# A hybrid attention and expert layer on one core: modulation rows, earlier head turns, products with diagonals, and one gather per tile

## The chip, the cores and the metric

The kernel runs on one core of a Trainium2 chip. The metric is device time in microseconds of one execution, the median of several. A profiled execution has a time of its own, which is given beside its span. The engines are TensorE (PE, and PEld for its weight loads), VectorE (DVE), ScalarE (ACT), GpSimd (POOL) and the DMA queues, which SyncE (SP), ScalarE and GpSimd issue.

## What is computed

One layer on 512 tokens of width 1024, in float32. `rms_norm(x)` is scaled and shifted by rows of `ada = c @ w_ada + b_ada`, projected by `w_in`, and goes through two attentions: a windowed one with 8 query heads and 2 key heads of 64 (chunks of 64, a window of two chunks, a bias by distance, a sink), and a latent one with 8 heads of 96 over all earlier chunks. Both are softmax attentions. Then comes a product-key expert network over 16384 experts.

```python
ada = c @ w_ada + b_ada
shift1, scale1, gate1, shift2, scale2, gate2 = [t[:, None, :] for t in jnp.split(ada, 6, axis=-1)]
h = rms_norm(x, norm1_g) * (1.0 + scale1) + shift1
z = h @ w_in
...
p = jnp.exp(scores - m)
denom = jnp.sum(p, axis=-1, keepdims=True) + jnp.exp(sink - m)
o = jnp.einsum('bckgqs,bcskd->bcqkgd', p / denom, vb)        # windowed
...
p = jax.nn.softmax(s, axis=-1)                               # latent, v alike
...
mix = jnp.concatenate([out_a, out_b], axis=-1).astype(x.dtype) @ w_out
x = x + gate1 * mix
h2 = rms_norm(x, norm2_g) * (1.0 + scale2) + shift2
x = x + gate2 * peer_ffn(h2, peer_w_query, peer_sub_keys, peer_u, peer_v)
```

`peer_ffn` scores 8 heads of keys, takes the 16 best of 128 twice and the 16 best pairs, and sums `gelu(u_e . x) * v_e` over them with softmax weights.

## The kernel before

It is one hand-written program per engine. Each engine has its list of instructions, and semaphores join them (`wait_ge`, `then_inc`); the order within an engine is the order in which the code is written. An engine that waits holds back all that stands behind it.

**Start.** SP loads c, x and then the weights in chunks of 512 columns (2 MB): first the modulation chunks 2, 3, 0 and 1 (`ada_order`), then the chunks of `w_in`. Chunks 2, 0 and 1 are `prepared`: DVE multiplies them by c and sums over the rows of 128 (`modulate`, L1243 and L1245), and PE sums over partitions (`modulation`, L874). Chunk 3 is `direct`: PE multiplies its columns with c, 32 matmuls of one moving column (L885). GpSimd adds the squares of x (L523), PE sums them over partitions (L897), ACT takes the root (L598), DVE the reciprocal (L1232). DVE scales (L1266), ACT shifts (L601), and `z_tile` (L915) is the projection by `w_in`.

**Heads.** Per token tile tt of 128: `project` makes the latent queries and keys, ACT copies them, DVE rotates and norms them (`rope`, `sum_heads`, `norm_heads`, which ends with the gain multiply L1364), and `turn_heads` transposes them on PE, 4 heads to a bank of PSUM, two banks in turn, each copied by ACT (`copy_heads`, L661). `turn_queries` does the same for the windowed queries (L942, `copy_queries`).

**Attention** is a pipeline of 48 units: 16 windowed ones (one token tile, two heads, at most 256 keys) and then 32 latent ones (one token tile, one head, 128 to 512 keys). In pass u PE does `scores(u + 2)` (L1002 windowed, over 64 rows; L1005 latent, over 96), `transposes(u)` (L1015, one 128x128 tile per 128 keys and head: 2 or 4 in a windowed unit, 1 to 4 in a latent one, 56 and 80 in all) and `values(u - 1)` (L1032). DVE does `bias_and_max`, divides the exponentials by their sum in place (`scale_probs`, L1417 reciprocal and L1420 multiply) and copies the result out. ACT does the exponentials (L716) and copies the transposed tiles to SBUF (L726). GpSimd has nothing to do here.

**Keys and experts.** Key scores of four token tiles go to SBUF by ACT (L790); three of them (p = 1 to 3) go out to HBM through two buffers, so that the copy of p = 3 waits until that of p = 1 has left. Then come 128 tiles of the table u and 128 of v. ACT rounds each (`high`), GpSimd makes the rest for u (`low_u`, L539), and PE makes 24 matmuls of 352 columns (`dot`, L1145 to L1147). Meanwhile DVE searches the keys of p = 0, then of p = 1 to 3 (`search`), and between the steps of a search it makes dot products with 128 gathered rows (`row_dot`, L1516) for the last token tile. GpSimd issues these gathers (L552) between its `low_u`; seven row buffers are there, and a gather waits until DVE has used the row seven before it (`row_used`). At u tile 28 PE turns the result of the search of p = 1 (`turn_slots`, L1163, which waits for DVE) and then builds gates (L1156) for 16 tiles. The rule for gathers is:

```python
while g < 2 * SU and (row_step[g - NROWS] <= m - 2 if g >= NROWS else m >= S0 + 3 + g):
    gather(g)
```

Of the kernel before, what the change touches and what calls it, by code (L numbers as in the profile page):

```python
# [59 lines left out]
def build(nc, xT, c, positions, position_cols, w_ada, b_ada, norm1_g, norm2_g, w_in, swa_q_norm, swa_k_norm,  # L60
          swa_sinks, mla_q_a_norm, mla_kv_a_norm, mla_w_uq, mla_w_ukv, mla_q_norm, mla_k_norm,
          w_out, peer_w_query, sub_keys, u_tiles, u_rows, v_tiles, outT):
    ctx = ExitStack()
    with ctx:
# [7 lines left out]
        def region(start, entries):  # L72
# [12 lines left out]
        (res, ident, ones, iota, cT, b_cols, ada, g1, g2, gs, eps), at0 = region(BASE, [  # L85
# [3 lines left out]
            ("g1", [P, KD], F32), ("g2", [P, KD], F32), ("gs", [P, KD], F32), ("eps", [P, 1], F32)])  # L89
# [16 lines left out]
            ("g_mla", [P, 2, QK], F32), ("trig", [P, TT, 2, ROPE // 2], F32), ("posq", [P, TT], I32),  # L106
# [11 lines left out]
        accs = m2[:].rearrange("p a h d -> p (a h d)")[:, 1024:2048].rearrange("p (a c) -> p a c", a=2)  # L118
        zsq_k = qkT[:].rearrange("p a t -> p (a t)")[:, 0:TT * P].rearrange("p (t c) -> p t c", t=TT)
# [25 lines left out]
        sout = (sout0, sout1)  # L145
# [55 lines left out]
        ms1 = sem("ms1")  # L201
        sd1 = sem("sd1")
        ada_done = sem("ada_done")
        ada_read = sem("ada_read")
        h_scaled = sem("h_scaled")
# [29 lines left out]
        p_ready = sem("p_ready")  # L235
        pt_ps = sem("pt_ps")
# [83 lines left out]
        direct = [ada_order[1]]  # L320
# [5 lines left out]

        def chunk(n):
            at = slot[n][0]
            return ring[at][:] if at < 3 else spare[at - 3]

        NSMALL = 12
# [83 lines left out]
        def _(sp):  # L415
# [38 lines left out]
            for p in range(1, TT):  # L454
                sp.wait_ge(s_copied, p + 1)
                sp.dma_start(keys[p], sout[p % 2][:].rearrange("p a n -> p (a n)")).then_inc(s_out[p % 2], 16)
# [51 lines left out]
        def _(pool):  # L508
            nc.gpsimd.memset(eps[:], EPS)
# [24 lines left out]

            sum_squares(rstd2[:], h2T, sq2, sq2_sum, KD - 1)
# [31 lines left out]
        def _(act):  # L567
# [20 lines left out]
            act.dma_start(g_mla[:, 0, :], mla_q_norm.partition_broadcast(P)).then_inc(small_in, 16)  # L588
            act.dma_start(g_mla[:, 1, :], mla_k_norm.partition_broadcast(P)).then_inc(small_in, 16)
# [8 lines left out]
            nc.scalar.activation(rstd1, ps[:, 6, :], ACT.Sqrt, bias=eps[:], scale=1.0 / D).then_inc(sd1, 1)  # L598
            for k in range(KD):
# [1132 lines left out]
```

## Time and profile before

| what | value |
|---|---|
| median of 3 runs | 1495.8 us (1495.46 to 1496.79) |
| profiled execution, its own time | 1498.02 us |
| its span | 1496.2 us |
| PE busy, share of the span | 1416.0 us, 95% |
| DVE, ACT, POOL busy | 1223.2, 707.6, 740.8 us |
| mean granted TensorE clock | 0.968 |

The span runs from the first to the last instruction. PEclk is the TensorE clock that was granted, as a share of 2.4 GHz; 0.50 is 1.2 GHz. Ends of matmuls are modelled, so that pieces of PE overlap in the rows; starts are what to go by.

### The profile page before, as it was taken

The page shows a single profiled execution, that of the slowest core. Times are in us where ns is not written, and L with a number is a line of the kernel's source. Part 1 is how long each engine was busy: PE and PEld are TensorE (multiplying, and loading weights), DVE is VectorE, ACT ScalarE, POOL GpSimd, SP SyncE. Part 2 cuts the span into 40 slices and gives each one's busy share as a digit, 9 for nine tenths or more (in the row PEclk, how much of TensorE's full clock was granted, in tenths as well). Part 3 has the DMA queues.
Part 4 walks back from the last instruction along what each step waited for, and adds up shares of the span by engine and source line. Part 5 has one row for each costly group of instructions (what it writes and reads, how often), then busy time and mean ns, then how long its engine had stood idle before and what let it go on. Part 6 is the DMA issues. An engine that isn't in the chain of part 4 may idle for free.

```text
span 1496.2 us, 23503 instructions
## 1 busy us (share of the span) xinstructions
PE 1416.0 (95%) x8439; PEld 1309.5 (88%) x8439; DVE 1223.2 (82%) x2649; ACT 707.6 (47%) x1311; POOL 740.8 (50%) x472
## 2 busy tenths in 40 slices
PE   3899899989897999989999999899999999999999
PEld 2564566768897999989999998899999999999998
DVE  3867667865779988958898886569999999999997
ACT  2234546332542688448853883343344334443342
POOL 2001000020467878768777776855555555565540
PEclk9999559999998999999999999999999999999999
DMA  8740100263569999999999999989999999999996
GB/s 319 278 147 1 57 1 1 80 234 137 189 224 333 319 330 334 358 380 321 325 345 402 329 332 351 412 288 372 391 396 386 395 392 391 389 393 392 391 390 228
DMA packets 158259, 438.88 MB, mean 293 GB/s; under 512 B 16768, under 2 KB 50880, under 8 KB 156992
## 3 DMA queue, kind: packets, MB, share of 16 engines
q1 hardware_dynamic: 91488, 244.55, 45.4%
q0 software_dynamic: 46080, 167.79, 29.4%
q10 hardware_dynamic: 20576, 25.05, 4.7%
q8 instruction: 67, 1.10, 0.3%
q14 instruction: 48, 0.39, 0.1%
HBM read 390.11 MB, written 47.22 MB: 292 GB/s over the span
## 4 chain that ended last, share of the span: by engine, by line
PE 75%; DVE 11%; DMA 5%; POOL 5%; ACT 2%; issue 2%; ACTq 0%; SPq 0%; DVEq 0%; POOLq 0%
PE ps L1196 11%; PE ps L1197 11%; PE ps L1198 11%; PE ps L1145 6%; PE ps L1146 6%; PE ps L1147 6%; PE ps L1156 5%; PE ps L915 4%; POOL lo L539 3%; PE ps L1032 2%; DMA raw<-in_u_tiles 2%; PE ps L1002 2%; PE ps L1015 2%; PE ps L1005 1%; POOL row_res L552 1%
## 5 line engine op out<-in xcount | busy, mean ns | idle before, releaser
L779 ACT ACTIVATE hi<-raw 128x1024 fp32r<-128x1024 f32 x256 | 271.2, 1060 | 312.0 <-PE ps L1198 221.7
L539 POOL TENSOR_TENSOR lo<-raw,hi 128x1024 fp32r<-128x1024 f32 x122 | 294.3, 2418 | 146.7 <-ACT hi L779 139.8
L1145 PE MATMUL ps<-h2hi,hi 128*128 128x352 f32 x1024 | 340.2, 332 | 26.2 <-POOL lo L539 17.2
L1146 PE MATMUL ps<-h2lo,hi 128*128 128x352 f32 x1024 | 334.8, 327 | 0.0
L1147 PE MATMUL ps<-h2hi,lo 128*128 128x352 f32 x1024 | 334.3, 327 | 0.0
L1197 PE MATMUL ps<-clo,hi 128*128 128x352 f32 x1008 | 324.1, 322 | 0.0
L1196 PE MATMUL ps<-chi,hi 128*128 128x352 f32 x1008 | 324.1, 322 | 0.0
L1198 PE MATMUL ps<-chi,lo 128*128 128x352 f32 x1008 | 324.1, 322 | 0.0
L1145 PEld LDWEIGHTS ps<-h2hi,hi 128*128 128x128 f32 x1024 | 196.4, 192 | 30.0 <-POOL lo L539 19.2
L552 POOL DMA_INDIRECT row_res<-in_v_tiles,E x91 | 149.9, 1647 | 137.3 <-DVE y_tok L1651 105.8
L1147 PEld LDWEIGHTS ps<-h2hi,lo 128*128 128x128 f32 x1024 | 196.2, 192 | 0.0
L1146 PEld LDWEIGHTS ps<-h2lo,hi 128*128 128x128 f32 x1024 | 196.1, 192 | 0.0
L1196 PEld LDWEIGHTS ps<-chi,hi 128*128 128x128 f32 x1008 | 189.3, 188 | 0.0
L1198 PEld LDWEIGHTS ps<-chi,lo 128*128 128x128 f32 x1008 | 189.3, 188 | 0.0
L1197 PEld LDWEIGHTS ps<-clo,hi 128*128 128x128 f32 x1008 | 189.3, 188 | 0.0
L1638 DVE TENSOR_TENSOR lo<-raw,hi 128x1024 fp32r<-128x1024 f32 x128 | 156.4, 1222 | 20.4 <-issue 10.0
L552 POOL DMA_INDIRECT rows<-in_v_tiles,E x69 | 111.6, 1617 | 84.1 <-DVE y_tok L1651 68.3
L803 ACT ACTIVATE act_out<-ps 128x352 f32<-128x352 f32 x128 | 59.2, 463 | 148.9 <-PE ps L1147 113.2
L1516 DVE SCALAR_TENSOR_TENSOR row_res<-row_res,ps 128x1024 f32<-128x1024 f32 x91 | 108.7, 1215 | 11.0 <-DMA row_res<-in_u_rows,E 5.8
L552 POOL DMA_INDIRECT row_res<-in_u_rows,E x91 | 90.5, 995 | 38.8 <-DVE row_res L1516 18.5
L814 ACT ACTIVATE ohW<-eqI,wS 128x128 f32<-128x128 f32 x352 | 107.4, 391 | 0.0
L1651 DVE SCALAR_TENSOR_TENSOR y_tok<-row_res,cc,y_tok 128x1024 f32<-128x1024 f32 x72 | 92.2, 1280 | 1.9
(286 smaller groups left out, 2216.2 us busy)
## 6 DMA issues: line engine op xcount, KB each, us to landing
raw<-in_u_tiles SPq DMA_DIRECT2D x128, 512.0 KB
raw<-in_v_tiles SPq DMA_DIRECT2D x128, 512.0 KB
gelus<-act_out ACTq DMA_DIRECT2D x128, 176.0 KB
act_in<-gelus SPq DMA_DIRECT2D x128, 176.0 KB
gates<-stage SPq DMA_DIRECT2D x32, 512.0 KB
gate<-gates SPq DMA_DIRECT2D x32, 512.0 KB
late<-in_w_ada SPq DMA_DIRECT2D x4, 2048.0 KB, 8.5
qkT<-in_w_ada SPq DMA_DIRECT2D x3, 2048.0 KB, 14.3
```

Of the source, the lines that this page charges most:

```text
L539: nc.gpsimd.tensor_tensor(lo[m % 3][:], raw[m % 3][:], hi[m % 3][:].bitcast(F32), ALU.subtract).then_inc(u_lo, 1)
L552: nc.gpsimd.indirect_dma_start(rows[g % NROWS], None, table, bass.IndirectOffsetOnAxis(ap=at, axis=0)).then_inc(row_in[g % NROWS], 16)
L779: nc.scalar.activation(hi[m % 3][:], raw[m % 3][:], ACT.Copy).then_inc(t_hi, 1)
L814: last = nc.scalar.activation(ohW[half][:, t, :], eqI[:, half, t, :], ACT.Copy, scale=wS[:, col:col + 1])
L1145: nc.tensor.matmul(out, hi[n % 3][:, cols], dense(h2hi, k), start=(k == 0), stop=False)
L1146: nc.tensor.matmul(out, hi[n % 3][:, cols], dense(h2lo, k), start=False, stop=False)
L1147: last = nc.tensor.matmul(out, lo[n % 3][:, cols], dense(h2hi, k), start=False, stop=(k == KD - 1))
L1196: nc.tensor.matmul(out, hi[m % 3][:, cols], chi[n % 4][:], start=(n == 0), stop=False)
L1197: nc.tensor.matmul(out, hi[m % 3][:, cols], clo[n % 4][:], start=False, stop=False)
L1198: last = nc.tensor.matmul(out, lo[m % 3][:, cols], chi[n % 4][:], start=False, stop=False)
L1516: nc.vector.scalar_tensor_tensor(out=row, in0=row, scalar=1.0, in1=x_tok, op0=ALU.mult, op1=ALU.mult, accum_out=aa[:, g:g + 1]).then_inc(r ...
L1638: tt_(lo[m % 3][:], raw[m % 3][:], hi[m % 3][:].bitcast(F32), ALU.subtract).then_inc(v_lo, 1)
```

## The change

There are seven edits.

1. **Modulation rows.** Chunks 3 and 1 (`direct`) are now multiplied by PE as rows: c is the stationary operand (one column), and 512 columns of the chunk move, 8 matmuls for a chunk. ACT copies the row to SBUF, and four matmuls of one row and one column turn it into columns. DVE prepares chunks 2 and 0 alone. The sum of squares comes first on PE. DVE computes the scale as soon as chunks 2 and 3 are there, and scales six of eight parts before it waits for the shift.
2. **Tables.** ACT loads the tables for Sqrt and Gelu with a one-element activation ahead of their use.
3. **Heads turned sooner.** `turn_heads(1)` stands ahead of `z_tile(0, 3)`, and the scores of units 0 and 1 ahead of the last turns. The gain of the latent heads is multiplied in ACT's copy of the turned queries, not by DVE.
4. **Products with diagonals.** DVE inverts the sums only. GpSimd writes `ident * (1 / sum)`, one 128x128 tile per head, and PE multiplies the exponentials with it by ordinary matmuls where it transposed.
5. **Key copies.** p = 1, 2 and 3 have a buffer each, so ACT's copies wait for no transfer.
6. **Gathers.** At most one per u tile until tile 28, at most three from there.
7. The modulation of `gate1` and `scale2` on DVE is moved behind the attention, and the Gelu of the gathered sums on ACT (L855) one tile later.

```diff
-        direct = [ada_order[1]]
+        direct = [ada_order[1], ada_order[3]]
...
+            def diagonals(u):
+                kind = units[u][0]
+                pool.wait_ge(r_ready, u + 1)
+                if u >= 2:
+                    pool.wait_ge(pt_ps, u - 1)
+                for j in range(heads_of(kind)):
+                    last = nc.gpsimd.tensor_scalar(diag[:, u % 2, j, :], ident[:], rsm[:, u % 4, j:j + 1], None, ALU.mult)
+                last.then_inc(p_ready, 1)
...
-                while g < 2 * SU and (row_step[g - NROWS] <= m - 2 if g >= NROWS else m >= S0 + 3 + g):
+                most = g + (1 if m < build_at[1] else 3)
+                while g < min(2 * SU, most) and (row_step[g - NROWS] <= m - 2 if g >= NROWS else m >= S0 + 3 + g):
...
+            act.wait_ge(eps_ready, 1)
+            nc.scalar.activation(spent[:, 0:1], eps[:], ACT.Sqrt)
             act.wait_ge(x_in, 16)
...
+            for j in direct:
+                act.wait_ge(ada_row, direct.index(j) + 1)
+                nc.scalar.activation(ada_rows(j), row_ps(j), ACT.Copy).then_inc(ada_row_sb, 1)
+            act.wait_ge(shift_ready, 1)
...
             root_queries(2)
             copy_heads(0)
             copy_projections(3)
+            copy_heads(1)
             square_heads(2)
...
-                if p == 3:
-                    act.wait_ge(s_out[1], 16)
-                to = s if p == 0 else sout[p % 2]
+                to = s if p == 0 else sout[p]
...
-                if n == more_at:
+                if n == more_at + 1:
...
-            def modulation_direct(j):
+            def modulation_row(j):
 
                 n = place["ada", j]
                 arrived(n)
+                for k in range(KD):
+                    last = nc.tensor.matmul(row_ps(j), cT[:, k:k + 1], chunk(n)[:, k, :], start=(k == 0), stop=(k == KD - 1))
+                last.then_inc(ada_row, 1)
+
+            def modulation_turned(j):
+
+                pe.wait_ge(ada_row_sb, direct.index(j) + 1)
                 for q in range(CH // P):
                     col = j * (CH // P) + q
...
+                    last = nc.tensor.matmul(ada_at(col), ada_rows(j)[:, q * P:(q + 1) * P], ones[0:1, 0:1],
+                                            start=True, stop=True)
...
-                    last = nc.tensor.transpose(ps[:, 4 + u % 2, slot * P:(slot + 1) * P],
-                                               p_view(u, kind)[:, j, c0:c0 + P], ident[:])
+                    last = nc.tensor.matmul(ps[:, 4 + u % 2, slot * P:(slot + 1) * P], p_view(u, kind)[:, j, c0:c0 + P],
+                                            diag[:, u % 2, j, :], start=True, stop=True)
...
+                if k == 5:
+                    modulation(0, 4)
+                    dve.sem_inc(shift_ready, 1)
...
-            def scale_probs(u):
+            def invert_sums(u):
                 kind, b, _, _ = units[u]
                 dve.wait_ge(exp_done, u + 1)
                 nj = heads_of(kind)
-                nk = len(key_tiles(kind, b)) * P
-                settled(nc.vector.reciprocal(rsm[:, u % 4, 0:nj], sm[:, u % 4, 0:nj]))
-                for j in range(nj):
-                    v = pb[:, u % 4, j, 256 - nk:256] if kind == "s" else p_view(u, kind)[:, 0, 0:nk]
-                    last = nc.vector.tensor_scalar(v, v, rsm[:, u % 4, j:j + 1], None, ALU.mult)
-                last.then_inc(p_ready, 1)
+                nc.vector.reciprocal(rsm[:, u % 4, 0:nj], sm[:, u % 4, 0:nj]).then_inc(r_ready, 1)
```

On TensorE the program began with these matmuls: L874 sums a prepared chunk over partitions (`ones` with the sums `m`), L897 is the sum of squares, L885 the direct chunk with `cT`, L915 the first projection.

```order
L874 MATMUL ps<-ones,m_75 128x1 x4
L897 MATMUL ps<-pb,ones 128x512
L885 MATMUL ps<-cT,ring_61 128x1 x32
L874 MATMUL ps<-ones,m_75 128x1 x8
L915 MATMUL ps<-ring_62,hT 128x512 x24
```

Now the sum of squares (L940) stands first, the row products (L922, with output 1x512) ahead of each prepared chunk (L913), and the turns of the rows (L930) behind it:

```order
L940 MATMUL ps<-pb,ones 128x512
L922 MATMUL ps<-ring_62,cT 1x512 x8
L913 MATMUL ps<-ones,m_76 128x1 x4
L930 MATMUL ps<-ones,pb 128x1 x4
L922 MATMUL ps<-qkc,cT 1x512 x8
L913 MATMUL ps<-ones,m_76 128x1 x4
L930 MATMUL ps<-ones,pb 128x1 x4
L961 MATMUL ps<-ring_63,hT 128x512 x24
```

32 matmuls of one column have become two times 8 matmuls of 512 columns, and one of three prepared chunks is gone.

On TensorE from the projections of the last token tile on (L955 and L961), the order was: the turns of heads 0, the projection, a `w_in` tile (L915), turns of heads (L970) and queries (L942), then scores (L1002) and transposes of exponentials `pb` (L1015).

```order
L970 MATMUL ps<-ident,m_75 96x128 x16
L955 MATMUL ps<-wuq,qkc 128x512 x2
L955 MATMUL ps<-wuq,qkc 128x256 x2
L961 MATMUL ps<-wukv,qkc 128x512 x2
L915 MATMUL ps<-ring_61,hT 128x512 x8
L970 MATMUL ps<-ident,m_75 96x128 x16
L942 MATMUL ps<-ident,z 128x128 x12
L970 MATMUL ps<-ident,m_late 96x128 x16
L942 MATMUL ps<-ident,z 128x128 x4
L970 MATMUL ps<-ident,m_late 96x128 x16
L1002 MATMUL ps<-qkc 128x128 x6
L1015 MATMUL ps<-ident,pb 128x128 x2
```

Now the second group of head turns (L1016, for L970) stands ahead of the `w_in` tile (L961), four matmuls of scores (L1042) ahead of the last turns, the turns of queries are L988, and the products with the diagonals (in `m_76`) are L1055:

```order
L1016 MATMUL ps<-ident,m_76 96x128 x16
L1001 MATMUL ps<-wuq,qkc 128x512 x2
L1001 MATMUL ps<-wuq,qkc 128x256 x2
L1007 MATMUL ps<-wukv,qkc 128x512 x2
L1016 MATMUL ps<-ident,m_76 96x128 x16
L961 MATMUL ps<-ring_62,hT 128x512 x8
L988 MATMUL ps<-ident,z 128x128 x12
L1016 MATMUL ps<-ident,m_late 96x128 x16
L1042 MATMUL ps<-qkc 128x128 x4
L988 MATMUL ps<-ident,z 128x128 x4
L1016 MATMUL ps<-ident,m_late 96x128 x16
L1042 MATMUL ps<-qkc 128x128 x2
L1055 MATMUL ps<-m_76,pb 128x128 x2
```

On GpSimd, around u tiles 19 to 22 (`lo` is the rest of a tile, the DMA rows are gathers; buffer numbers tell the tiles apart), the order was one gather after each tile and then eight in a row behind the fourth of these:

```order
L539 TENSOR_TENSOR lo_143<-raw_137,hi_140 128x1024
L552 DMA row_res_152<-in_u_rows,E 128x1024
L539 TENSOR_TENSOR lo_144<-raw_138,hi_141 128x1024
L552 DMA row_res_153<-in_u_rows,E 128x1024
L552 DMA rows_147<-in_u_rows,E 128x1024
L552 DMA rows_148<-in_u_rows,E 128x1024
L552 DMA rows_149<-in_u_rows,E 128x1024
L552 DMA row_res_150<-in_u_rows,E 128x1024
L552 DMA row_res_151<-in_u_rows,E 128x1024
L552 DMA row_res_152<-in_u_rows,E 128x1024
L552 DMA row_res_153<-in_u_rows,E 128x1024
L539 TENSOR_TENSOR lo_142<-raw_136,hi_139 128x1024
```

Now one gather follows each tile here too:

```order
L568 TENSOR_TENSOR lo_145<-raw_139,hi_142 128x1024
L581 DMA row_res_154<-in_u_rows,E 128x1024
L568 TENSOR_TENSOR lo_146<-raw_140,hi_143 128x1024
L581 DMA row_res_155<-in_u_rows,E 128x1024
L568 TENSOR_TENSOR lo_144<-raw_138,hi_141 128x1024
L581 DMA rows_149<-in_u_rows,E 128x1024
L568 TENSOR_TENSOR lo_145<-raw_139,hi_142 128x1024
L581 DMA rows_150<-in_u_rows,E 128x1024
L568 TENSOR_TENSOR lo_146<-raw_140,hi_143 128x1024
```

The seven gathers that are left over at tile 28 are made up for by three at each of tiles 28 to 31.

## Rows read from the trace of the kernel before

**Rows 1.** Stretches: start:end, length; PE, PEld, DVE, ACT, POOL busy; PEclk, DMA share, GB/s.

```profile
24.00:36.00 12.00, 10.26 (x43) 9.26 (x43) 5.74 (x5) 1.97 (x2) 0.00 (x0) 1.00 1.05 389
146.00:165.90 19.90, 12.71 (x77) 10.78 (x76) 12.23 (x27) 14.30 (x30) 0.00 (x0) 0.75 0.18 59
165.90:216.00 50.10, 50.09 (x188) 30.96 (x188) 31.35 (x110) 21.19 (x69) 0.00 (x0) 0.50 0.05 19
216.00:275.80 59.80, 59.18 (x339) 38.63 (x337) 44.11 (x170) 39.17 (x115) 0.00 (x0) 0.99 0.01 1
387.60:510.60 123.00, 112.03 (x682) 111.17 (x681) 113.15 (x443) 50.87 (x66) 86.07 (x49) 0.96 0.81 288
```

**Rows 2.** The page's chain that ended last, shares by engine.

```profile
PE 75%; DVE 11%; DMA 5%; POOL 5%; ACT 2%; issue 2%; ACTq 0%; SPq 0%; DVEq 0%; POOLq 0%
```

**Rows 3.** Timeline of the start: start us, us, engine, line, operation.

```profile
12.21 8.74 POOL L523 TENSOR_TENSOR pb<-pb,hT 128x512 f32<-128x512 f32 x6
17.68 0.49 DVE L1243 TENSOR_SCALAR m<-ring,cT 128x512 f32<-128x512 f32 x1 [17.68 <-DMA ring<-in_w_ada]
29.28 13.65 PE L885 MATMUL ps<-cT,ring 128*128 128x1 f32 x64
29.57 1.28 ACT L598 ACT_TABLE_LOAD   x1 [15.74 <-PE ps L897]
51.74 23.39 PE L915 MATMUL ps<-ring,hT 128*128 128x512 f32 x48 [2.37 <-ACT hT L601]
56.14 0.34 PEld L915 LDWEIGHTS ps<-ring,hT 128*128 128x128 f32 x1 [0.52 <-ACT hT L601]
56.95 0.19 PEld L915 LDWEIGHTS ps<-ring,hT 128*128 128x128 f32 x1 [0.47 <-issue]
```

**Rows 4.** Timeline of TensorE around the last turns.

```profile
157.92 1.08 PE L970 MATMUL ps<-ident,m_late 128*96 128x128 f32 x8 [1.77 <-DVE m_late L1364]
165.91 0.69 PE L1015 MATMUL ps<-ident,pb 128*128 128x128 f32 x2 [1.80 <-DVE pb L1420]
```

**Rows 5.** Busy time of each engine, two stretches of the turns.

```profile
149.40:152.40 3.00, 3.00 (x15) 2.94 (x15) 2.14 (x4) 1.78 (x4) 0.00 (x0) 0.50 0.00 0
152.40:155.80 3.40, 2.86 (x26) 2.52 (x25) 1.74 (x4) 3.04 (x9) 0.00 (x0) 0.99 0.00 0
```

**Rows 6.** Groups by line, 180 to 212 us: times, count, busy, mean.

```profile
L1002 PE MATMUL ps<-qkc 64*128 64x256 f32 x32 | 16.8, 671 | 0.0
L1032 PE MATMUL ps<-m,z 128*64 128x128 f32 x64 | 9.0, 435 | 0.0
L1015 PE MATMUL ps<-ident,pb 128*128 128x128 f32 x32 | 8.9, 434 | 0.0
```

**Rows 7.** Busy of L1015, then of L1156: PE, PEld, clock, DMA share, GB/s.

```profile
240.00:270.00 30.00, 7.32 (x48) 6.14 (x48) 1.00 0.01 1
510.00:600.00 90.00, 29.82 (x246) 29.48 (x247) 1.00 0.95 327
```

**Rows 8.** Timeline of GpSimd at the start.

```profile
1.57 0.29 POOL L515 TENSOR_SCALAR_AFFINE_SELECT ident<-ident 128x128 f32<-128x128 f32 x1 [0.17 <-POOL ident L513]
```

**Rows 9.** Timeline of the key stage, ScalarE and TensorE.

```profile
390.19 2.06 ACT L790 ACTIVATE sout<-ps 128x512 f32<-128x512 f32 x4 [2.68 <-DMA keys<-sout]
402.25 0.43 PE L1145 MATMUL ps<-h2hi,hi 128*128 128x352 f32 x1 [1.87 <-POOL lo L539]
```

**Rows 10.** Timeline, 448 to 511 us, of VectorE and TensorE.

```profile
448.16 1.22 DVE L1516 SCALAR_TENSOR_TENSOR rows<-rows,ps 128x1024 f32<-128x1024 f32 x1 [7.97 <-DMA rows<-in_u_rows,E]
480.87 0.66 PE L1145 MATMUL ps<-h2hi,hi 128*128 128x352 f32 x1 [8.35 <-POOL lo L539]
507.75 2.21 DVE L1565 TENSOR_TENSOR IJW<-eW,eR 128x128 f32<-128x128 f32 x1
510.62 0.49 PE L1163 MATMUL ps<-ident,IJW 128*128 128x128 f32 x3
```

**Rows 11.** Timeline of ScalarE near 974 us.

```profile
974.27 0.34 ACT L855 ACTIVATE cc<-aa 128x160 f32<-128x160 f32 x1 [0.40 <-ACT act_out L803]
```

More of the change, by code:

```diff
@@ L82, in region @@
             return out, at
[L85 removed]
+        (res, ident, ones, iota, cT, b_cols, ada, g1, g2, gs, eps, spent), at0 = region(BASE, [
             ("res", [P, KD, T], F32),
@@ L325, in acc, with ada_at, row_ps, ada_rows @@
             return (accs_late if j in (6, 7, 10, 11) else accs)[:, prepared.index(j) % 2, :]
+        def ada_at(col):
+            return ps[:, 3, col:col + 1] if col < KD else ada_ps[:, col:col + 1]
+        def row_ps(j):
+            return ps[0:1, 4 + direct.index(j), :]
+        def ada_rows(j):
+            at = T * (1 + direct.index(j))
+            return pb[:].rearrange("p a j k -> p (a j k)")[0:1, at:at + CH]
         def chunk(n):
@@ L533, in _ @@
                                       z[:, tt, Z_KR:Z_KR + ROPE].unsqueeze(1).to_broadcast([P, MH, ROPE])).then_inc(m_built, 1)
+            def diagonals(u):
[6 more added lines that the diff above has]
+                last.then_inc(p_ready, 1)
+            for u in range(NU):
+                diagonals(u)
             sum_squares(rstd2[:], h2T, sq2, sq2_sum, KD - 1)
@@ L694, in _ @@
             square_heads(3)
-            copy_heads(1)
-            for tt in range(3):
+            for tt in range(2):
                 copy_queries(tt)
@@ L768, in _ @@
             high_w(("query", 1))
+            nc.scalar.activation(spent[:, 2:3], eps[:], ACT.Gelu)
             for h in range(PH):
@@ L841, in _ @@
                     gelu(n)
+                    if i == 0 and p == 1:
+                        act.wait_ge(s_out[1], 32)
                     if i == 0 and p >= 2:
@@ L1034, in values @@
                 last.then_inc(o_ps, 1)
+            for tt in range(3):
+                turn_queries(tt)
+            turn_heads(2)
             scores(0)
             scores(1)
+            turn_queries(3)
+            turn_heads(3)
+            pe.wait_ge(mt_sb, 4 * TT)
+            pe.wait_ge(zq_sb, TT)
             for u in range(NU):
@@ L1305, in _ @@
                 settled(nc.vector.memset(distm[0:64, b, 192:256], MASKED))
-            for j in prepared[3:7]:
+            for j in prepared[2:6]:
                 modulate(j)
@@ L1432, in copy_out @@
                 ins.then_inc(o_sb, 1)
-            for piece in (2, 4):
-                modulation(piece, 8)
-            settled(nc.vector.scalar_tensor_tensor(out=gs[:], in0=ada[:, 4 * KD:5 * KD], scalar=1.0, in1=g2[:],
-                                                   op0=ALU.add, op1=ALU.mult))
             bias_and_max(0)
@@ L1450, in low_w @@
                 tt_(wlo[:], chunk(place[key]), whi[:].bitcast(F32), ALU.subtract).then_inc(w_split, 1)
+            for piece in (2, 4):
+                modulation(piece, 8)
+            settled(nc.vector.scalar_tensor_tensor(out=gs[:], in0=ada[:, 4 * KD:5 * KD], scalar=1.0, in1=g2[:],
+                                                   op0=ALU.add, op1=ALU.mult))
             for k in range(KD):
```

75 lines of the change are left out of this document (37 added, 38 removed).

## The prediction

> **What bounds the kernel now.** I read the page's chain of waits first [rows 2]: TensorE has 75% of it, DVE 11%, transfers and GpSimd 5% each. So a change counts where it shortens TensorE's work, raises its clock, or removes a wait of it. Then I read the stretches that the edits touch, with the clock in each [rows 1]. The reader is to see three kinds. From 165.9 to 216 us TensorE is busy for 50.09 of 50.10 us, with the clock at 0.50, and DVE (31.35) and ScalarE (21.19) have room: these are 14 of the 16 windowed units, and what sets them is the clock. From 216 to 275.8 the clock is 0.99 and TensorE is still full (59.18 of 59.80). From 146 to 165.9 (12.71 of 19.90), and from 387.6 to 510.6 (112.03 of 123, DVE 113.15), TensorE waits for others. Last I read single rows of the start, the last turns, the keys and the gathers in time order [rows 3, 4, 9, 10].
>
> The profiled execution took 1498.0 us, 2.2 above the median; all sums are made against it and then lowered by 2.2.
>
> **Start.** The first modulation chunk lands at 17.68 and DVE works on it at once [rows 3]. A chunk has 2.1 MB, and 389 GB/s [rows 1] give 5.4 us each, so the second is there at about 25 to 27 and the fourth near 36. The direct chunk takes 13.65 us from 29.28 [rows 3], so the projection starts at 51.74. A product of 512 columns: the projection's 24 take 23.39 us; up to 56.95 a weight load is 0.34 us long, from then 0.19 [rows 3], so 5.2 us at half speed are three products of 1.73, and the other 21 are 0.87 each. A row of 8 is thus 13.8 us at half speed and 6.9 at full. I take a rise after three products: row one from 27 to 38, its turn until 39.5, row two 39.5 to 46.5, then the sum, the turn and DVE's copy until 48, and ScalarE's shift, for which the projection waits now too (2.37) [rows 3]: 48.9, so −2.8. The first eight products then run at full speed: 6.9 for 3×1.73+5×0.87=9.6, −2.7. **Start −5.5.** The table load of 1.28 us at 29.57 lies inside it. From below: both rows at full speed, which chunk four at 36 limits to 1 or 2 us more, −7. From above: no rise, +10 (a rival).
>
> **Heads sooner.** The turns wait 1.77 us for the gain multiply of DVE, which ScalarE's copy now does, and unit 0's first transpose waits 1.80 for its softmax [rows 4]; the scores of units 0 and 1 now come ahead of the last turns. At most both waits go, −3.6. Against it, ScalarE is busy for 14.30 of the 19.90 us [rows 1] and keeps its copies in order, so that it can be 0. **I take half, −1.8.**
>
> **Windowed units.** 32 us hold 8 units [rows 6], 4.0 each: scores 16.8/8=2.1, values 1.13, four transposes of 0.278. At full clock a transpose is 7.32/48=0.1525 [rows 7]. A product of 128×128 is not in this place; the nearest is the gates' L1156, two records each: 29.82/123=0.242 at full clock [rows 7], so 0.485 at half. It is dearer by 0.207 at half clock and 0.09 at full. First the row on the clock: in 149.4 to 152.4 TensorE did nothing but turns, without a gap, and the clock went from 0.50 to 0.99 behind it [rows 5]. So transposes raise it. But in 165.9 to 216 TensorE was as full and the clock stayed low [rows 1]; there scores and values, over 64 rows or 64 columns, fill 3.2 of 4.0 us. What the products change is the part of a pass that works on 128 rows and 128 columns: 4×0.278=1.1 of 4.0 becomes 4×0.485=1.94 of 4.8. That is a reason for an earlier rise, no proof. I take it after seven passes: four with two tiles, 4×2×0.207=+1.7; three with four, 3×4×0.207=+2.5; seven at full clock, 2.1/2+4×0.242+1.13/2=2.6 for 4.0, −9.8 to −10.5 (the pieces overlap; I take 2.5); the last two, at full clock already, 2×4×0.09=+0.7. **Windowed units −5.6.** Who makes the diagonals: a 128×128 select took GpSimd 0.29 us [rows 8], the two-source adds 8.74/6=1.46 for 512 columns [rows 3], 0.36 for 128, so two are 0.6 to 0.7 us of a pass. DVE loses its multiplies. This lies beside TensorE: a unit's softmax has two passes, 5.0 us.
>
> The Trainium skill ("Perfetto Trace Analysis", section "Transposes") says that a turn should be made by transpose and not by a standard matmul, since a transpose skips arithmetic. The trace agrees in size, 0.1525 against 0.242 a tile [rows 7]; by that rule alone 136 tiles would cost 136×0.09=+12 us at full clock, and the edit would be a loss.
>
> **Latent units.** They run at full clock with TensorE full [rows 1]. The units of token tiles 1 to 3 have 8×(2+3+4)=72 tiles, times 0.09: **+6.5**. The eight of tile 0 have one tile each and wait for ScalarE, so nothing.
>
> **Keys.** ScalarE waits 2.68 us for the transfer that frees its buffer, and the first u tiles then wait 1.87 for GpSimd [rows 9], which works behind ScalarE. Own buffers remove the first wait; at TensorE I take the second, **−1.9** (0 to −2.7).
>
> **Tables.** The root ahead of norm 2 and the Gelu ahead of its use have other work on ScalarE beside them: **−0.1**.
>
> **Gathers.** Eight gathers in a row on GpSimd make TensorE wait 8.35 us at u tile 21 [rows 10]. From tile 3 at 402.25 [rows 9] to the start of that wait, 480.87−8.35=472.5, are 18 tiles, 3.9 each; without it tile 28 would be reached at 499.8 and not at 510.62. That is 10.8: the wait, and 2.5 of low clock behind it. But the turn of the slots at tile 28 waits for DVE, whose search ends at 507.75+2.21=509.96 [rows 10], and DVE is busy for 113.15 of 123 us [rows 1]. So TensorE loses the same time later, queued behind L1163 with all products of u. DVE's first row product waited 7.97 for its row [rows 10], and gathers come at one per tile now, so DVE isn't faster either. **I take +1**, for a cold clock behind the new wait; bounds −3 (the 2.21 us of the last add, which is long beside a busy GpSimd, become short) and +3.
>
> **Row sums one tile later.** L855 waits 0.40 at 974.27 [rows 11] and goes one tile of 3.9 back. DVE's use of it follows: 0 to +3.9, hidden if DVE has time there. **+1.** The moved modulation is cheap DVE work in stretches in which TensorE is full: 0.
>
> Sum: −5.5 −1.8 −5.6 +6.5 −1.9 −0.1 +1 +1 = **−6.4**, 1491.6 for this execution, 1489.4 as a median. The bounds of the terms together give it −15 to −1.
>
> **Rivals.**
> *The clock stays at 0.50 through the windowed units.* For it: 50 us of full TensorE did not raise it. Then +1.7, 10×4×0.207=+8.3 and +0.7, 10.7 for −5.6: the sum is +9.9, 1505.7. It decides from the third pass at half clock more than forecast on: each costs 0.83+1.5=2.3, so from 3 passes more the gain is gone. This ends on the other side.
> *The clock is up from the first unit.* Four small passes ((50.1−10×4.0)/4=2.5 now, with dearer products 2.9) fall to DVE's 31.35/14=2.24, −2.7, and three from 4.8 to 2.5, −7: sum −16.1, 1479.7. For it: the turns ahead of them raised the clock [rows 5], and the gap from 155.8 to 165.9 gets shorter. Against it, a gap remains, and the clock fell in it. By the Trainium skill ("TensorE: Matmul & The Clock Gate", "Part 4: PE-mode transpose") transposes do not count as work for the clock, and products would; rows 5 speak against the first half.
> *Rows of one output partition leave the clock low.* Each row is then 13.8 us, the projection starts near 62 and its first tile is cold as now: start +10 for −5.5, sum +9.1, 1504.9. The direct matmuls of one column before the projection left it at half speed too [rows 3].
> *Both bad ones:* +25.4, 1521.
> *The wait at tile 21 is won in full:* −10.8 for +1, sum −18.2, 1477.6. This needs DVE's search to end 10 us sooner.
>
> **How the numbers follow.** Forecast 0.42, clock low in the windowed units 0.18, rows slow 0.17, clock up from the first unit 0.12, both bad 0.07, gathers won 0.04. A measurement of this kernel tells some 0.2%, 3 us, from no change. The likeliest case alone has 1481 to 1495, a seventh of it within 3 us of 1495.8. Lower cases and the two middle rivals' edges give faster 0.56, same 0.11, slower 0.33. The range 1475 to 1507 leaves out the double case and the tails of the others.
>
> **What would show it.** In the changed profile: the projection at 48 to 50 us (62 if rows are slow); the products with diagonals 0.24 us each at full clock; the stretch from unit 0 to unit 15 some 6 us shorter, with the clock going up in its middle; GpSimd's diagonals 0.3 us; from 240 us on each latent unit longer by its tiles times 0.09; no wait at u tile 21 and one of near 10 us before L1163's successor at tile 28. The prediction is wrong if the clock's rise lies elsewhere, which is its weakest step, or if DVE's search moves. Diagonals above 1.2 us would fill a pass of 2.5.

## The result and the profile after

| | before | changed |
|---|---|---|
| median, beside each other | 1495.63 us (4 executions) | 1505.43 us (4: 1503.04, 1503.45, 1507.41, 1519.88) |
| the changed kernel a second time | 1496.98 us (19) | 1509.11 us (6: 1502.01 to 1522.62) |
| profiled execution, own time | 1498.0 us | 1503.04 us |
| PE, DVE, GpSimd busy | 1416.0, 1223.2, 740.8 us | 1420.5, 1191.8, 782.0 us |

The ratio is 1.0083, 95% interval 1.0052 to 1.0113, and 1.0104 (1.0065 to 1.0142) the second time. The kernel became slower by about 10 us. Its profiled execution is one of the fastest and is 5.0 us longer than the profiled one of before, in time and in span (1501.2 to 1496.2), so two things have to be found: where these 5 us come from, and why most executions are longer still.

The chain of waits of the changed kernel, by engine, shows no new bound: TensorE's share is 79% for 75% [rows 2] (72% in the second profiled execution of the same kernel, that of experiment 10).

```profile
PE 79%; DMA 7%; POOL 4%; DVE 4%; ACT 2%; issue 2%; SPq 1%; ACTq 0%; POOLq 0%; DVEq 0%
```

The difference came from setting the same points of the two traces side by side. The starts are those of TensorE's first matmul there; for unit 47 it is the last of its transposes or products.

| point | before | changed | difference | added in between |
|---|---|---|---|---|
| projection (L915, now L961) | 51.74 | 45.19 | −6.55 | −6.55 |
| unit 0's first product | 165.91 | 158.27 | −7.64 | −1.1 |
| unit 16's (first latent) | 219.87 | 208.24 | −11.63 | −4.0 |
| unit 47's last | 273.35 | 271.9 | −1.4 | +10.2 |
| u tile 0 | 387.60 | 387.35 | −0.25 | +1.2 |
| u tile 4 | 406.99 | 407.95 | +0.96 | +1.2 |
| u tile 29 | 516.49 | 522.73 | +6.2 | +5.3 |
| end of the span | 1496.2 | 1501.2 | +5.0 | −1.2 |

First the start, in TensorE's timeline. The first row takes 8.37 us, the second 7.03, at full speed for most of it, and the 24 products of the projection take 20.84 in place of 23.39 [rows 3].

```profile
24.20 8.37 PE L922 MATMUL ps<-ring,cT 128*1 128x512 f32 x16 [1.61 <-DMA ring<-in_w_ada]
35.04 7.03 PE L922 MATMUL ps<-qkc,cT 128*1 128x512 f32 x16 [0.51 <-DMA qkc<-in_w_ada]
45.19 20.84 PE L961 MATMUL ps<-ring,hT 128*128 128x512 f32 x48 [1.16 <-ACT hT L636]
```

Next the last turns of heads and queries ahead of unit 0. TensorE is full for 6.8 us at a clock of 0.50 there, where the kernel before has 3.4 us of it (columns of the first line as in [rows 1]), and the first product waits 2.97 us for its diagonal, where the first transpose waited 1.80 for DVE [rows 4].

```profile
146.40:153.20 6.80, 6.80 (x31) 5.39 (x29) 2.95 (x9) 3.31 (x6) 0.00 (x0) 0.50 0.00 0
...
146.04 1.67 PE L1016 MATMUL ps<-ident,m_late 128*96 128x128 f32 x8 [3.34 <-ACT qkT L696]
158.27 1.23 PE L1055 MATMUL ps<-m,pb 128*128 128x128 f32 x4 [2.97 <-POOL m L558]
```

Then the attention by stretches (columns as in [rows 1]). The clock is at 0.50 for five units, and at 1.00 from somewhere in unit 5 on. In the last stretch, the latent units, TensorE is still full, and it lasts 63.7 us where it lasted 53.5 (219.87 to 273.35).

```profile
158.20:176.50 18.30, 18.23 (x60) 12.28 (x60) 7.00 (x24) 6.82 (x25) 5.90 (x11) 0.50 0.16 60
181.10:208.20 27.10, 25.52 (x195) 19.39 (x195) 16.56 (x56) 14.39 (x46) 11.23 (x19) 1.00 0.01 2
208.20:271.90 63.70, 63.13 (x371) 45.31 (x371) 29.86 (x123) 35.47 (x105) 18.67 (x31) 1.00 0.00 1
```

What one product costs is read from starts, since ends are modelled. In a latent unit with three tiles, the changed kernel's timeline has the three products at 242.41 and the next group at 243.18, so 0.77/3=0.257 each.

```profile
242.41 0.83 PE L1055 MATMUL ps<-m,pb 128*128 128x128 f32 x6
243.18 0.87 PE L1072 MATMUL ps<-m,kvm 128*64 128x128 f32 x6
```

In the kernel before, the same place gives 0.42/3=0.140.

```profile
252.92 0.49 PE L1015 MATMUL ps<-ident,pb 128*128 128x128 f32 x3
253.34 0.87 PE L1032 MATMUL ps<-m,kvm 128*64 128x128 f32 x6
```

GpSimd's instruction for a diagonal, in the answer on its line, takes 0.60 us and not 0.3, and TensorE waited for it 32 times, 16.7 us in all (most of it a weight load's wait, with matmuls still running beside it; the second line is from the answer on L1055):

```profile
L558 POOL TENSOR_SCALAR m<-ident,rsm x64: 592/602/610, 157.0 to 269.6; 128x128 f32<-128x128 f32 x64
...
  POOL m L558: 16.7, 32
```

Last the u tiles. The chain there goes through four engines, so rows of all of them are needed. TensorE waits 5.07 us at tile 22 and 7.13 at tile 28; ScalarE waits 8.70 for the tile itself; SyncE had issued nothing between 459 and 469.57; GpSimd, whose gathers stand behind its `lo`, issues none between 470.46 and 482.48; and DVE later waits 4.74 for a row.

```profile
482.39 0.66 PE L1192 MATMUL ps<-h2hi,hi 128*128 128x352 f32 x1 [5.07 <-POOL lo L568]
515.39 0.90 PE L1210 MATMUL ps<-ident,IJW 128*128 128x128 f32 x3 [7.13 <-DVE IJW L1607]
...
478.84 1.06 ACT L818 ACTIVATE hi<-raw 128x1024 fp32r<-128x1024 f32 x1 [8.70 <-DMA raw<-in_u_tiles]
...
454.97 4.17 SPq L461 DMA_DIRECT2D raw<-in_u_tiles  x2
469.57 0.33 SPq L495 DMA_DIRECT2D s<-keys  x1
469.94 23.86 SPq L461 DMA_DIRECT2D raw<-in_u_tiles  x7
...
470.46 0.95 POOL L581 DMA_INDIRECT rows<-in_u_rows,E  x1
479.98 2.36 POOL L568 TENSOR_TENSOR lo<-raw,hi 128x1024 fp32r<-128x1024 f32 x1 [8.57 <-ACT hi L818]
482.48 0.95 POOL L581 DMA_INDIRECT rows<-in_u_rows,E  x1
...
487.91 1.22 DVE L1558 SCALAR_TENSOR_TENSOR rows<-rows,ps 128x1024 f32<-128x1024 f32 x1 [4.74 <-DMA rows<-in_u_rows,E]
```

What stands at 469.57 is the load of the next token tile's keys into `s`. SyncE waits for DVE to have read the old ones (`s_free`), and every u tile that comes after in its queue waits along. The kernel before has the same rows; I had not read SyncE's queue:

```profile
457.84 0.33 SPq L444 DMA_DIRECT2D raw<-in_u_tiles  x1
468.54 0.33 SPq L478 DMA_DIRECT2D s<-keys  x1
468.91 24.36 SPq L444 DMA_DIRECT2D raw<-in_u_tiles  x6
```

Behind GpSimd's burst of gathers there was thus a second wait: experiment 4 moves it alone. Theory 1, before any experiment: the products lose in the latent units and win in the windowed ones according to the moment at which the clock rises; DVE's search sets tile 28, and one gather a tile makes its rows, and so the search, late. The rivals stand with the experiments.

### The profile page after: what moved, and what is told of

Its sections match the earlier page's. It is cut to its first block, busy times and chain, and to the rows that moved or that the text cites. A ratio compares the mean times of both kernels' runs of the same rounds, so it can differ in the third digit from the quotient of the medians.

```text
span 1501.2 us, 23763 instructions
## 1 busy us (share of the span) xinstructions
PE 1420.5 (95%) x8551; PEld 1309.7 (87%) x8551; DVE 1191.8 (79%) x2573; ACT 707.7 (47%) x1315; POOL 782.0 (52%) x536
## 4 chain that ended last, share of the span: by engine, by line
PE 79%; DMA 7%; POOL 4%; DVE 4%; ACT 2%; issue 2%; SPq 1%; ACTq 0%; POOLq 0%; DVEq 0%
PE ps L1244 11%; PE ps L1245 11%; PE ps L1243 11%; PE ps L1192 8%; PE ps L1194 7%; PE ps L1193 7%; PE ps L1203 5%; PE ps L961 4%; DMA row_res<-in_u_rows,E 2%; POOL lo L568 2%; DMA raw<-in_u_tiles 2%; PE ps L1055 2%; PE ps L1072 2%; DMA qkc<-in_w_ada 1%; PE ps L1045 1%
## 5 line engine op out<-in xcount | busy, mean ns | idle before, releaser
L581 POOL DMA_INDIRECT row_res<-in_v_tiles,E x91 | 155.0, 1704 | 135.0 <-DVE y_tok L1693 101.8
L1558 DVE SCALAR_TENSOR_TENSOR rows<-rows,ps 128x1024 f32<-128x1024 f32 x69 | 82.8, 1216 | 18.4 <-DMA rows<-in_u_rows,E 17.9
```

The lines of the kernel that those rows point to most:

```text
L581: nc.gpsimd.indirect_dma_start(rows[g % NROWS], None, table, bass.IndirectOffsetOnAxis(ap=at, axis=0)).then_inc(row_in[g % NROWS], 16)
L1558: nc.vector.scalar_tensor_tensor(out=row, in0=row, scalar=1.0, in1=x_tok, op0=ALU.mult, op1=ALU.mult, accum_out=aa[:, g:g + 1]).then_inc(r ...
```

## The experiments

Each kernel was timed in five rounds beside the kernel before, on one chip for each group of four; its medians there are 1496.62 us (1 to 4), 1495.25 (5 to 8) and 1496.98 (9 to 12).

**1. Products taken out.** Transposes and DVE's multiplies are back in all units.

```diff
-                    last = nc.tensor.matmul(..., p_view(u, kind)[:, j, c0:c0 + P], diag[:, u % 2, j, :], start=True, stop=True)
+                    last = nc.tensor.transpose(..., p_view(u, kind)[:, j, c0:c0 + P], ident[:])
```

> The changed kernel with the transposes and DVE's multiplies back in all 48 units; all else stays changed. Theory 1 (the products lose in the latent units 0.117 us a tile and win in the windowed ones only as far as the clock rises): in the profile the latent units go back from 63.6 to about 54 us, the windowed ones from 50 to about 54 at a clock of 0.50; the time is near 1494 to 1497 us, some 6 to 10 below the changed kernel. Rival (the products pay, and the loss is all at the u tiles): the time is 1506 or more.

Measured: 1499.27 us (12), 6 to 10 below the changed kernel's two medians. The latent units take 53.5 us, the windowed ones 55.2, at a clock of 0.50 for 50 of them:

```profile
160.10:210.30 50.20, 50.14 (x188) 30.97 (x189) 31.46 (x111) 21.13 (x68) 0.00 (x0) 0.50 0.08 29
```

The attention was 4.6 us ahead of before at its end, but 4.4 behind at tile 29, where it had waited for DVE's search for 10.9 us. That is why the time lies above the range that was expected.

**2. The old gathers.** Only the rule for gathers is undone.

> The changed kernel with the old rule for gathers alone. Theory 1 (one gather a tile delays DVE's rows, and with them the search whose end u tile 28 waits for): tile 28 starts 4 to 6 us earlier counted from tile 4, the wait before u tile 22 is again about 8 us, the wait before the turn of the slots goes to under 2 us, and the time is about 5 us below the changed kernel. Rival (the loss there comes from the changed phase and not from the gathers): tile 28 stays where it is, within 1.5 us.

Measured: 1502.1 us (8), 3 and 7 below the changed kernel's two medians. From tile 4 to tile 29 it takes 111.6 us, and 114.8 in the changed kernel, 109.5 before. The waits changed places as expected: 8.5 us before a u tile, 1.3 before the turn of the slots. These are TensorE's waits in the u tiles of the changed kernel and, below, of this one (total, times, longest):

```profile
PE ps L1192 <- POOL lo L568: 7.6, 2, 5.1
PE ps L1210 <- DVE IJW L1607: 7.1, 1, 7.1
```

```profile
PE ps L1191 <- POOL lo L568: 10.6, 2, 8.5
PE ps L1209 <- DVE IJW L1606: 1.3, 1, 1.3
```

3.2 us of the 5.3 belong to the rule; the expectation said 4 to 6.

**3. Products in the windowed units alone.** `by_product` is `[u for u in range(NU) if units[u][0] == "s"]`.

> The changed kernel with products in the 16 windowed units and transposes in the 32 latent ones. Theory 1: latent units 9 to 10 us shorter than in the changed kernel, the windowed ones as they are in it (50 us if the clock rises at unit 6, up to 65 if it doesn't), so about 9 us below the changed kernel in every run. If the products in the windowed units pay for themselves, it is also below the kernel with transposes in all units run beside it; if the rise of the clock is late in most executions, it is above it.

Measured: 1493.23 us (12), beside 1499.27 for transposes in all units and 1496.62 before (30). The latent units are 10.2 us shorter than in the changed kernel. So the windowed products pay about 6 us in the middle of their executions (5.5 in the profiled ones: unit 16 comes 49.65 us after unit 0 for 55.15), but 2 of the 12 took 1501.4 and 1511.7, with mean clocks of 0.973 and 0.966 where the others have 0.975 to 0.978.

**4. The load of keys later.**

```diff
-                    if m == search_at[p - 1] + 10:
+                    if m == search_at[p - 1] + (10 if p == 1 else 12):
```

> The changed kernel with SyncE's load of the next key scores (which waits for DVE and holds the loads of u tiles behind it) two tiles later, for p = 2 and 3. Theory 1 (SyncE's queue, not the gathers, makes u tile 22 wait; and DVE's search sets tile 28): the wait of 5.1 us before tile 22 goes, the wait before the turn of the slots grows by as much, and tile 28 and the time stay within 1.5 us of the changed kernel's. Rival (the wait at tile 22 is on the path): 4 to 5 us faster than the changed kernel. Second rival (the wait comes from elsewhere): the wait stays.

Measured: 1501.4 us (11). The wait at tile 22 is gone, and that at tile 28 has grown by 4.2:

```profile
PE ps L1210 <- DVE IJW L1607: 11.3, 1, 11.3
PE ps L1192 <- POOL lo L568: 2.3, 1, 2.3
```

So SyncE's queue was the cause, and DVE's search sets tile 28. The kernel gained more than expected: from tile 4 to 29 it takes 111.2 us for 114.8, since GpSimd was held up with the tiles, too, and issues its gathers in time now; DVE's wait of 4.74 is gone.

**5. Products alone**, on top of the kernel before (edit 4, all 48 units).

> The kernel before with the products and diagonals alone (edit 4), in all 48 units. Theory 1: latent units 9 to 10 us longer than in the kernel before, windowed units 4 to 5 us shorter where the clock rises in their first half and up to 10 longer where it doesn't, nothing lost at the u tiles beyond 1 or 2 us; so 1501 to 1503 us with some executions above 1510. Rival (all seven edits together lose the time, none alone): 1496 or less.

Measured: 1506.86 us (6: 1501.98 to 1518.48), ratio 1.0087 (1.0054 to 1.0119). Edit 4 alone costs about what the whole change lost; what the other edits give and take nearly cancels (experiments 2 and 11). Its profiled execution is a long one, 1514.1 us. The clock stays low for four units more, each 5.07 us long and not 2.9: with a first product at 164.0 it is still at 0.50 up to 202.5, and in the changed kernel, with a first product at 158.3, it is at 1.00 from 181.1 at the latest:

```profile
164.00:182.30 18.30, 18.28 (x61) 12.27 (x61) 6.99 (x24) 6.83 (x25) 5.87 (x10) 0.50 0.09 35
182.30:202.50 20.20, 20.20 (x81) 14.70 (x80) 7.53 (x24) 6.30 (x20) 4.74 (x8) 0.50 0.01 2
202.50:222.00 19.50, 18.42 (x135) 14.31 (x135) 10.87 (x38) 9.61 (x31) 7.71 (x13) 0.93 0.01 1
```

**6. Matmuls with the identity**, on top of the kernel before: no diagonals, DVE's multiplies stay.

```diff
-                    last = nc.tensor.transpose(..., ident[:])
+                    last = nc.tensor.matmul(..., ident[:], start=True, stop=True)   # windowed units
```

> The kernel before with the 56 windowed transposes made as ordinary matmuls with the identity; DVE's multiplies stay and GpSimd has nothing to do. If the longer matmuls themselves bring the clock up (theory 1), it rises at about unit 6 here too, the windowed units take about 50 us and the time is 3 to 5 us below the kernel before, 1492. Rival (the shorter chain without DVE's multiplies, or the other edits around, bring it up): the clock stays at 0.50 to unit 13 or so, the windowed units take 62 to 65 us, and the time is near 1505.

Measured: 1491.03 us (12), ratio 0.9980 (0.9956 to 1.0003). The clock rises in unit 6, and the windowed units take 50.2 us:

```profile
162.20:185.50 23.30, 23.27 (x80) 15.95 (x80) 12.93 (x47) 8.59 (x32) 0.00 (x0) 0.50 0.13 49
185.50:212.40 26.90, 26.63 (x195) 20.50 (x195) 21.62 (x75) 14.45 (x46) 0.00 (x0) 0.94 0.01 2
```

So what raises the clock sooner is the matmul in place of the transpose, not the shorter chain. The gain in time, 4.2 us by medians, is not quite clear of noise, since the interval just takes in 1. At full clock a unit takes 2.74 us here, every one; with GpSimd's diagonals they take 2.74 and 3.06 in turn.

**7. A version from these:** products in the windowed units alone, keys two tiles later, first gathers a tile sooner, fewer rows in the first search.

```diff
-        FILL, PAUSES, EARLY, MORE = {1: 15, 2: 9, 3: 9}, 15, 4, 4
+        FILL, PAUSES, EARLY, MORE = {1: 10, 2: 11, 3: 12}, 15, 4, 4
...
-                while ... else m >= S0 + 3 + g):
+                while ... else m >= S0 + 2 + g):
```

> The changed kernel with products in the windowed units alone, the load of the next key scores two tiles later, the first gathers one tile sooner, and 10, 11 and 12 rows in the three searches in place of 15, 9 and 9. Theory 1 (DVE's search sets u tile 28): no wait before tiles 21 to 23, the wait before the turn of the slots under 3 us, tile 28 at about 106 us after tile 4 less 8, and the time 8 to 12 us below the hybrid kernel's 1493, so 1482 to 1486. Rival (the rows come due later, in the searches p = 2 and 3): the gain at tile 28 is given back by tile 96, and the time is near 1493.

Measured: 1482.1 us (6), ratio 0.9920 (0.9898 to 0.9943). Of TensorE's waits in the u tiles one is left:

```profile
PE ps L1202 <- POOL lo L571: 2.4, 1, 2.4
```

Tile 28 stands 93.1 us after tile 4, 108.0 in the changed kernel: more than the 8 of the expectation.

**8. Fewer rows in the first search**, the line `FILL` of experiment 7 alone, on the changed kernel.

> The changed kernel with 10, 11 and 12 rows in the three searches in place of 15, 9 and 9, nothing else. Theory 1 (DVE's search sets u tile 28): tile 28 comes 6 to 10 us earlier counted from tile 4 (five row products of 1.2 us, and waits for rows), with the wait of about 5 us at tile 22 still there; the time is 5 to 8 us below the changed kernel's if the later searches have room, unchanged if not. Rival (gathers or transfers set it): tile 28 stays within 2 us.

Measured: 1501.43 us (12). Tile 28 comes 97.0 us after tile 4 in place of 108.0. The wait at tile 22 is gone as well, since DVE reaches the end of the old keys sooner (SyncE issues the load at 464.51 and not at 469.57), and tile 28 still waits 4.0 us:

```profile
PE ps L1210 <- DVE IJW L1607: 4.0, 1, 4.0
PE ps L1192 <- POOL lo L568: 2.6, 1, 2.6
```

From tile 29 to the end it takes 982.3 us, 3.7 more than the changed kernel: the rows that were moved cost a third of the gain later.

**9. Tile 3 ahead of the last key store.**

```diff
             for p in range(1, TT):
+                if p == TT - 1:
+                    load_tile(3)
                 sp.wait_ge(s_copied, p + 1)
```

> The changed kernel with SyncE's load of u tile 3 ahead of the last store of key scores (it stood behind it and waited with it for ScalarE's copies). Theory 1 (the wait at u tile 3 is SyncE's queue and not ScalarE's wait for a key buffer): tile 3's load is issued some 3 us sooner, the wait of 2.5 us before tile 3 goes and with it 1 to 3 us of low clock at tiles 3 and 4, so tile 4 starts 3 to 6 us sooner after tile 0; at tile 28 DVE's search still rules, so less than 2 us of it stay at the end. Rival (the wait is GpSimd's or ScalarE's): the wait stays within 1 us.

Measured: 1502.97 us (8). The wait at tile 3 is gone, tile 4 starts 16.3 us after tile 0 in place of 20.6, and tile 28 waits for DVE again, 11.3 us. From tile 4 to 29 it takes 118.1. Of the 4.3 us, 3.3 are given back there.

**10. The changed kernel again.**

> The changed kernel once more, unaltered, for its distribution. Theory 1 (the unit at which the clock rises differs between executions and one pass at half clock costs 1.75 to 2 us): single executions spread over 15 us or more, the longer the lower their mean clock (0.977 at 1503, 0.966 at 1520), more than those of the kernel before, and the median lies at 1503 to 1507. Rival (the first four were an accident): a spread under 8 us.

Measured: 1509.11 us (6): 1502.0, 1506.6, 1507.2, 1511.0, 1515.4, 1522.6, with mean clocks of 0.977, 0.976, 0.977, 0.974, 0.970, 0.966. The 19 of the kernel before lie between 1491.5 and 1499.8. The median was above the expectation, the spread as it said. For the longest the size fits: a mean of 0.966 over 1520 us is 2×0.034×1520=103 us at half clock, 0.977 over 1503 is 69, and 34 us more at half clock cost 17. For the middle ones it does not: 1506.6 and 1507.2 have 0.976 and 0.977, hardly less than the 0.977 of 1503.0. The execution of 1506.6 was profiled, and its clock rises in the sixth unit, too; its units take what they take in the first profile:

```profile
159.90:178.10 18.20, 18.20 (x60) 12.24 (x60) 7.00 (x24) 6.82 (x25) 5.84 (x10) 0.50 0.16 58
182.30:209.40 27.10, 25.50 (x195) 19.39 (x195) 16.58 (x56) 14.41 (x46) 11.27 (x19) 1.00 0.01 2
...
519.19 0.90 PE L1210 MATMUL ps<-ident,IJW 128*128 128x128 f32 x3 [10.41 <-DVE IJW L1607]
```

It is 3.5 us longer than that profile for other reasons: unit 0 starts 1.6 us later, mostly because its first projection products are at half clock, and from tile 4 to 29 it takes 117.7 us for 114.8, with a wait of 10.4 for DVE's search.

**11. Everything but the products and the gathers.**

> The changed kernel with transposes and DVE's multiplies in all units and the old rule for gathers: edits 1, 2, 3, 5 and 7 alone. Theory 1 (start and heads win 7 to 8 us, keys nothing, the rest within 2): attention and norm 2 end 4 to 6 us sooner than before (the clock's rise at the end of the windowed units may move by a pass), and the time is 2 to 7 us below the kernel before, 1489 to 1494. Rival (DVE's search absorbs what comes before it): within 1.5 us of before.

Measured: 1493.73 us (12), ratio 0.9980 (0.9967 to 0.9993), 3.3 below before, so the start's gain stays. From experiment 1 it differs by the rule for gathers alone, and is 5.5 us below it; from tile 4 to 29 it takes 111.1 us where that one takes 119.3.

**12. All that gained.** As experiment 7, with matmuls by the identity for the diagonals in the windowed units and tile 3 first.

> All that gained: edits 1, 2, 3, 5 and 7; ordinary matmuls with the identity in the windowed units and transposes in the latent ones, DVE's multiplies in all; the load of the next keys two tiles later, tile 3's load ahead of the last key store, first gathers a tile sooner, rows 10, 11 and 12. Theory 1: 2 to 5 us below the 1482 of the kernel with diagonals in the windowed units, since a pass is 2.74 us without GpSimd and 2.9 with it (10 passes) and tile 3 comes sooner; so 1477 to 1481. Rival (the diagonals were worth their wait, DVE's multiplies cost more): 1482 or above.

Measured: 1477.32 us (6: 1472.68 to 1480.28), ratio 0.9868 (0.9846 to 0.9890): 19.7 us below the kernel before. Attention and the first u tiles in stretches; from tile 0 to tile 28 and a little on, TensorE is busy for 115.26 of 116.30 us:

```profile
159.90:210.20 50.30, 50.03 (x274) 36.55 (x275) 34.56 (x122) 22.85 (x77) 0.00 (x0) 0.74 0.08 29
210.20:263.80 53.60, 53.37 (x292) 33.93 (x291) 40.67 (x154) 36.09 (x105) 0.00 (x0) 1.00 0.00 1
379.40:495.70 116.30, 115.26 (x726) 114.43 (x724) 111.87 (x444) 53.79 (x77) 87.80 (x47) 1.00 0.84 295
```

From experiment 7 it differs by two things, the identity matmuls and tile 3, 4.8 us together. They were not run apart there, but the profiled executions tell them apart: tile 4 stands 17.5 us after tile 0 for 20.6, and unit 16 comes 50.3 us after unit 0 for 49.8, since the clock rises in the seventh unit and not in the sixth. So the expected time came, but the identity matmuls, which it was put down to in the first place, gave nothing in this execution. What the first gathers a tile sooner give by themselves was not run.

## Why the prediction was wrong

It said 1489.4 us and faster; the kernel is slower by 10. In the profiled execution the sum was to be −6.4 and is +5.0, and the steps that missed most are the gathers (by 4.3 us), the latent units (3.7), the keys (3.1) and the windowed units (1.6). Term by term, by the profiled execution, and with what the experiments say of the others:

- **Start, −5.5: right in kind, too small.** The projection began at 45.19 and not at 48.9, and its first products run at full speed (−2.5 of the −2.7). Together −9.1. The rows did not keep the clock low. This execution was a lucky one: in the other profiled ones with the edit the first projection products run at half clock for some us again, the 24 take about as long as before (0.9 to 1.1 us less), and the start gives −6.3 to −7.7.
- **Heads, −1.8: not there.** Start and heads together are −7.6 at unit 0 here, and −5.2 to −6.0 in the other profiled executions with these two edits (unit 0 at 159.9 to 160.7). That −7.6 is near the −7.3 of the forecast is luck: the start gave more, and 0.7 to 1.7 us were lost again where 1.8 were to be won. The step that failed counted the two waits of 1.77 and 1.80 alone, and neither the clock nor the chain that the diagonals make longer. The clock is low for 6.8 us of full work before unit 0 where it was for 3.4, which is 1.7 us of work, and the first product waits 2.97 us for 1.80, because its diagonal comes from GpSimd; in experiment 11, with DVE's multiply, it is 2.21, and such kernels (1, 11, 12) lose 0.7 to 0.8 here, those with diagonals 1.5 to 1.7. No run took edit 3 apart, so why the clock falls sooner there is open.
- **Windowed units, −5.6: −4.0, and not a fixed size.** The step "I take it after seven passes" was a good guess for this execution (the clock rises in the sixth) and for seven other profiled ones; it did not for the profiled one of experiment 5 (the tenth), and mean clocks of 0.974 and less in five of the changed kernel's ten executions suggest that such ones are common. The forecast took one place for the rise, while the kernel had become one whose time depends on it: a pass at half clock costs 5.07 for 4.11 before, and at full clock 2.9 for the 2.5 that I had worked out, so each pass that it comes later costs 2.2 us. That sensitivity, and not the likeliest place, is what the chances should have carried. The rival "stays at 0.50" gave 1505.7 with the clock low to the end, which no trace of a kernel with products shows; its number is near the median by accident.
- **Latent units, +6.5: +10.2. This step failed by its price.** 0.09 a tile came from busy times, in which overlapping pieces are merged; starts give 0.257−0.140=0.117. 72×0.117=8.4, and the eight units of token tile 0, which I had at nothing, took 1.7 more, with GpSimd's diagonals of 0.60 in their chain. By this alone the sum of edit 4 was against it. The Trainium skill ("Perfetto Trace Analysis", section "Transposes") says so: a turn is to be a transpose. The trace agrees in the latent units, 10 us in experiment 3, and not in the windowed ones, where the products won 6 us by the clock.
- **Keys, −1.9: +1.2. The step failed that read GpSimd's wait as the key buffer's.** ScalarE's 2.68 us did go, but tile 3's load stood in SyncE's queue behind the last key store, was issued 2.7 us sooner (389.92 for 392.65) and then took 8.2 us to land where it took 6. Experiment 9 moves the load and the wait goes.
- **Gathers, +1: +5.3. The step failed that said "DVE isn't faster either", and left it the same.** The bound was rightly named, tile 28 waits for DVE's search. But the search ended 5.4 us later (515.34 for 509.96): at tile 22 SyncE's queue kept the tiles back for DVE itself, GpSimd waited with them with its gathers unissued, and DVE then waited for rows. With the burst of the old rule, its rows were on their way already. Experiments 2, 4 and 8 each take away one link and get 3.2, 3.6 and 10.8 us there.
- **The rest, +1: −1.2** from tile 29 on, and +1.2 between attention and u tile 0, which moves by as much among the kernels (113.9 to 115.7 us from unit 47's last to tile 0). It can't be put down to an edit: experiment 6, without the other edits, has 115.4.

The profiled sum is then −7.6−4.0+10.2+1.2+1.2+5.3−1.2=+5.1. What the median is above that is in part shown. Executions of 1511 us and more, and one of 1507.4, have mean clocks of 0.974 and less, and there a later rise is the likely cause, by the rows of experiment 5 and by the sizes in experiment 10; none of these was profiled for the changed kernel itself, and a low mean clock doesn't say where it was low: experiment 1, with transposes, has an execution of 1508.5 with 0.955. The one of 1506.6 that was profiled owes its 3.5 us to the start and to DVE's search. By medians, the products alone cost +11.6 (experiment 5), the rule for gathers +3 to +7 (experiments 2 and 11 against 1), the rest −3.3 (experiment 11); together +11 to +15, where the changed kernel has +9.8 and +12.1.

## What to carry to other kernels

Price an operation by the distance of starts in a full engine, not by merged busy times. Before taking a wait away, read who is late next, SyncE's queue included: two of the waits here were loads that stood behind a wait for something else in that queue, and moving the wait was worth more than the edit that seemed to remove it. When a gain hangs on a clock that rises at a varying moment, work out what one step later costs, and time the kernel often enough to see its spread.

## What the runs showed of the hardware

- In the same place and with the same 128×128 tiles, ordinary matmuls brought the clock from 0.50 to 1.00 in the sixth or seventh unit of ten profiled executions and in the tenth of one (experiment 5); transposes left it at 0.50 for 14 or more of the 16 (up to 217.3 us in the kernel before, and to 213.7 at least in experiment 11, shown here). The Trainium skill ("TensorE: Matmul & The Clock Gate", "Part 4: PE-mode transpose") says that transposes don't count as a matmul does, and here the trace leans to it; but transposes alone raised the clock in [rows 5], and the matmuls also run longer, which no run kept apart.

```profile
160.40:213.70 53.30, 53.30 (x204) 33.47 (x205) 33.25 (x117) 22.69 (x73) 0.00 (x0) 0.50 0.07 26
```

- A row of 8 products with one stationary column ran at full speed for most of it: 8.37 us for the first, 7.03 for the second. In the other profiled executions the first took up to 9.95.
- A multiply of a 128×128 tile by a column takes GpSimd 0.60 us, twice a select of that size [rows 8].
- Single executions of one kernel spread over 20 us (1502.0 to 1522.6) with products in all units, over 21 with products in the windowed ones (experiment 3) and 18 with identity matmuls (experiment 6), over 8 (experiment 11) to 15 (experiment 1) with transposes. In experiments 7 and 12, six executions each, it was under 8.
